# A third weight sum of a Winograd product made on VectorE instead of by a load and an accumulating DMA

## The reference, cut to what matters

```python
h = _rmsnorm(x, g_ffn[l])
z = _dwconv_centred(h @ w_up[l], conv_w[l], conv_b[l])      # w_up: 1024 x 5632
z_gate, z_val = jnp.split(z, [D_FF], axis=-1)               # D_FF = 2816, 22 tiles of 128
x = x + (jax.nn.silu(z_gate) * z_val) @ w_down[l]
```

## Time and profile before

| | us |
|---|---|
| median of 3 runs | 1084.41 (1084.4 to 1085.13) |
| the profiled execution | 1084.41 |
| its span, first to last instruction | 1082.6 |
| PE busy | 1071.1 (99%) |
| PEld busy | 941.5 (87%) |
| POOL busy | 636.1 (59%) |
| DVE busy | 596.6 (55%) |
| ACT busy | 557.4 (51%) |

### The profile page before, as it was taken

The page is one execution under the profiler, slowest core; times in us unless marked ns, Lnnn a source line. Parts: engine busy times, 40 slices in busy tenths (PEclk is TensorE's granted clock), DMA queues, the critical chain, the costliest instruction groups (busy, mean ns, idle before and its releaser), DMA issues.

```text
span 1082.6 us, 18370 instructions
## 1 busy us (share of the span) xinstructions
PE 1071.1 (99%) x6492; PEld 941.5 (87%) x6492; DVE 596.6 (55%) x922; ACT 557.4 (51%) x772; POOL 636.1 (59%) x314
## 2 busy tenths in 40 slices
PE   9999999999999999999999999999999999999997
PEld 7788888888899989998878888888879998899987
DVE  4735755677146730676636359556741776136664
ACT  7835334545266623675548344445444675257651
POOL 5333334344799948995634333434458995789940
PEclk9999999999999999999999999999999999999999
DMA  8232123232999459972522221322349973898512
GB/s 306 96 97 79 59 65 110 78 112 83 247 232 241 119 158 248 208 167 96 173 81 89 79 79 60 97 97 78 101 141 266 231 177 98 241 207 221 133 56 79
DMA packets 45156, 151.12 MB, mean 140 GB/s; under 512 B 5264, under 2 KB 8080, under 8 KB 45072
## 3 DMA queue, kind: packets, MB, share of 16 engines
q1 hardware_dynamic: 35152, 115.42, 32.9%
q0 software_dynamic: 9216, 33.56, 16.9%
q10 hardware_dynamic: 704, 1.07, 0.3%
HBM read 131.15 MB, written 2.10 MB: 123 GB/s over the span
## 4 chain that ended last, share of the span: by engine, by line
PE 70%; POOL 9%; DVE 9%; DMA 4%; ACT 3%; issue 3%; DVEq 0%; ACTq 0%; SPq 0%; POOLq 0%
PE acc L1482 12%; PE acc L1483 12%; PE acc L1484 12%; POOL w_lo L464 8%; PE acc L1796 7%; PE acc L1799 7%; PE acc L1798 7%; DVE arena L1304 3%; PE acc L1608 3%; PE acc L1610 3%; PE acc L1609 3%; DMA mixer_sb<-w_raw 2%; DMA w_raw<-slabs 2%; ACT arena L805 2%; DVE sides L1295 1%
## 5 line engine op out<-in xcount | busy, mean ns | idle before, releaser
L474 POOL TENSOR_TENSOR w_lo<-w_raw,w_hi 128x1024 fp32r<-128x1024 f32 x108 | 262.2, 2448 | 331.8 <-ACT w_hi L541 329.0
L464 POOL TENSOR_TENSOR w_lo<-w_raw,w_hi 128x1024 fp32r<-128x1024 f32 x72 | 190.7, 2752 | 37.4 <-ACT w_hi L824 24.7
L1482 PE MATMUL acc<-feat_hi,w_hi 128*128 128x512 f32 (+1 forms) x496 | 190.1, 383 | 1.6 <-DVE x L1246 1.5
L1483 PE MATMUL acc<-feat_lo,w_hi 128*128 128x512 f32 (+1 forms) x496 | 189.7, 382 | 0.0
L1484 PE MATMUL acc<-feat_hi,w_lo 128*128 128x512 f32 (+1 forms) x496 | 189.6, 382 | 0.0
L541 ACT ACTIVATE w_hi<-w_raw 128x1024 fp32r<-128x1024 f32 x102 | 107.9, 1063 | 139.8 <-PE acc L1484 103.4
L1798 PE MATMUL acc<-xg_lo,w_hi 128*128 128x256 f32 x512 | 144.9, 283 | 0.0
L1799 PE MATMUL acc<-xg_hi,w_lo 128*128 128x256 f32 x512 | 144.9, 283 | 0.0
L1796 PE MATMUL acc<-xg_hi,w_hi 128*128 128x256 f32 x512 | 144.9, 283 | 0.0
L1482 PE MATMUL acc<-xg_hi,w_hi 128*128 128x512 f32 x352 | 139.6, 397 | 0.0
L1483 PE MATMUL acc<-xg_lo,w_hi 128*128 128x512 f32 x352 | 137.1, 389 | 0.0
(11 more groups left out here) (179 smaller groups left out, 2136.6 us busy)
## 6 DMA issues: line engine op xcount, KB each, us to landing
w_raw<-slabs SPq DMA_DIRECT2D x166, 512.0 KB, 3.5
mixer_sb<-slabs SPq DMA_DIRECT2D x16, 512.0 KB, 5.6
w_raw<-slabs POOLq DMA_DIRECT2D x16, 512.0 KB, 6.7
arena<-slabs SPq DMA_DIRECT2D x16, 512.0 KB, 4.9
arena<-slabs POOLq DMA_DIRECT2D x16, 512.0 KB, 7.1
second_s<-slabs SPq DMA_DIRECT2D x8, 512.0 KB, 6.5
mixer_sb<-w_raw POOLq DMA_DIRECT2D x8, 512.0 KB, 8.8
w_raw<-mixer_sb POOLq DMA_DIRECT2D x8, 512.0 KB, 6.6
```

The lines of the kernel that those rows point to most:

```text
L464: pool.tensor_tensor(w_lo[:, w], source, w_hi[:, w].bitcast(F32), ALU.subtract).then_inc(lo_done, 1)
L474: pool.tensor_tensor(w_lo[:, w], w_raw[:, w], w_hi[:, w].bitcast(F32), ALU.subtract).then_inc(lo_done, 1)
L1482: pe.matmul(out, wh, ah, start=first, stop=False)
L1483: pe.matmul(out, wh, al, start=False, stop=False)
```

## The change

S2 is no longer made by DMA. SP's second load of A11 (`load_s2`) and POOL's accumulating DMA (`add_s2`) go, with the semaphores `s2_loaded` and `s2_added`. In their place DVE adds `raw1` and `raw0` into `s2_raw` with one `tensor_tensor` per quad, 16 in all, and increments `s2_done`. It waits until S1 is summed, A11 is loaded, and the quad two before has done with the same S2 buffer. POOL's `add_s3`, which overwrites A11, now waits for `s2_done`, and ACT's `high_s2` does too.

```diff
--- before.py
+++ after.py
@@ -271,8 +271,7 @@
         s1_added = [sem(f"s1_added{i}") for i in range(2)]
         s3_added = [sem(f"s3_added{i}") for i in range(2)]
         s4_added = [sem(f"s4_added{i}") for i in range(2)]
-        s2_loaded = [sem(f"s2_loaded{i}") for i in range(2)]
-        s2_added = [sem(f"s2_added{i}") for i in range(2)]
+        s2_done = sem("s2_done")
         e12_done, t1_raw_done, t2_done, t_raw_done = (sem("e12_done"), sem("t1_raw_done"), sem("t2_done"),
                                                       sem("t_raw_done"))
         t_hi_done, t_ready = sem("t_hi_done"), sem("t_ready")
@@ -341,20 +340,13 @@
                 def load_a22(s):
                     sp.dma_start(raw(3), block(s, 3)).then_inc(a22_loaded, 16)
 
-                def load_s2(s):
-                    sp.dma_start(s2_raw[s % 2], block(s, 0)).then_inc(s2_loaded[s % 2], 16)
-
                 def load_down(m):
                     sp.dma_start(raw(m % RING), block(KP, m)).then_inc(raw_loaded[m % RING], 16)
 
                 for j, load in enumerate((load_a11, load_a21, load_a12, load_a22)):
                     low_of(L, p, 0, j - RING)
                     load(0)
-                    if j == 0:
-                        sp.wait_ge(t1_ready, L + 1)
-                        load_s2(0)
                 load_a21(1)
-                load_s2(1)
                 load_a11(1)
                 load_a12(1)
                 for s in range(2, KP):
@@ -365,7 +357,6 @@
                     low_of(L, p, s - 2, S3_)
                     load_a11(s)
                     low_of(L, p, s - 2, S4_)
-                    load_s2(s)
                     load_a12(s)
                 low_of(L, p, KP - 2, S2_)
                 load_down(1)
@@ -480,23 +471,16 @@
                 pool.dma_start(raw1[s % 2], block_of(L * NS + first_slab(p, s) + 3),
                                accum_op=ALU.add).then_inc(s1_added[s % 2], 16)
 
-            def add_s2(L, p, s):
-
-                count = 16 * ((L * QUADS + p * KP + s) // 2 + 1)
-                pool.wait_ge(s2_loaded[s % 2], count)
-                pool.wait_ge(s1_added[s % 2], count)
-                pool.dma_start(s2_raw[s % 2], raw1[s % 2], accum_op=ALU.add).then_inc(s2_added[s % 2], 16)
-
             def add_s3(L, p, s):
 
                 low_done(L * NU + first_unit(p, s) + A11_)
+                pool.wait_ge(s2_done, L * QUADS + p * KP + s + 1)
                 pool.dma_start(raw0[s % 2], block_of(L * NS + first_slab(p, s) + 1),
                                accum_op=ALU.add).then_inc(s3_added[s % 2], 16)
 
             def add_s4(L, p, s):
 
                 low_done(L * NU + first_unit(p, s) + A12_)
-                pool.wait_ge(s2_added[s % 2], 16 * ((L * QUADS + p * KP + s) // 2 + 1))
                 pool.dma_start(raw2[s % 2], s2_raw[s % 2], accum_op=ALU.add).then_inc(s4_added[s % 2], 16)
 
             def low_quad(L, p, s):
@@ -509,8 +493,6 @@
                 low(n + A12_, raw2[s % 2])
                 add_s4(L, p, s)
                 low(n + S2_, s2_raw[s % 2])
-                if s < KP - 1:
-                    add_s2(L, p, s + 1)
                 low(n + A22_, raw(3))
                 low(n + S3_, raw0[s % 2])
                 low(n + S4_, raw2[s % 2])
@@ -525,7 +507,6 @@
                     low(n - 2, raw(2))
                     add_s1(L, p, 0)
                     low(n - 1, raw(3))
-                    add_s2(L, p, 0)
                     for s in range(KP):
                         low_quad(L, p, s)
                     down = at + first_unit(p, KP)
@@ -840,7 +821,7 @@
                     high(first_unit(p, s) + A12_, raw2[s % 2])
 
                 def high_s2(p, s):
-                    act.wait_ge(s2_added[s % 2], loads(p, s))
+                    act.wait_ge(s2_done, L * QUADS + (p * KP + s + 1))
                     high(first_unit(p, s) + S2_, s2_raw[s % 2])
 
                 def high_a22(p, s):
@@ -1318,6 +1299,17 @@
                 def halves(bank):
                     return bank.rearrange("p (r s) -> p r s", r=2)
 
+                def add_s2(p, s):
+
+                    count = 16 * (L * (QUADS // 2)) + 16 * ((p * KP + s) // 2 + 1)
+                    dve.wait_ge(s1_added[s % 2], count)
+                    dve.wait_ge(a11_loaded[s % 2], count)
+                    if p * KP + s > 1:
+                        before = p * KP + s - 2
+                        dve.wait_ge(s4_added[before % 2], 16 * (L * (QUADS // 2)) + 16 * (before // 2 + 1))
+                        dve.wait_ge(lo_done, L * NU + (first_unit(before // KP, before % KP) + S2_ + 1 + RING))
+                    dve.tensor_tensor(s2_raw[s % 2], raw1[s % 2], raw0[s % 2], ALU.add).then_inc(s2_done, 1)
+
                 def add_c11(p, s):
                     dve.wait_ge(acc_ready, L * NU + (first_unit(p, s) + A12_ + 1))
                     dve.wait_ge(copied, quad_at(p, s) * 4 + 2)
@@ -1364,7 +1356,7 @@
                 def quad_low(p, s, b):
                     feat_low(FIRST_TILES + p * KT + 2 * s + b, 2 * s + b, b)
 
-                def convolve(p, s):
+                def convolve(p, s, between):
 
                     add_c12(p, s)
                     scale(p, s, 0)
@@ -1373,6 +1365,7 @@
                     taps(p, s, 0)
                     scale(p, s, 3)
                     taps(p, s, 2)
+                    between()
                     gate(p, s, 0)
                     taps(p, s, 3)
                     quad_low(p, s, 0)
@@ -1381,7 +1374,9 @@
 
                 def quad_step(p, s):
                     if s:
-                        convolve(p, s - 1)
+                        convolve(p, s - 1, (lambda: add_s2(p, s + 1)) if s < KP - 1 else (lambda: None))
+                    else:
+                        add_s2(p, 1)
                     add_c11(p, s)
                     add_c22(p, s)
                     add_c21(p, s)
@@ -1397,12 +1392,18 @@
                 dve.wait_ge(t1_hi_done, L + 1)
                 dve.tensor_tensor(xg12_lo, t1_raw.rearrange("p (k s) -> p k s", k=KP), xg12_hi.bitcast(F32),
                                   ALU.subtract).then_inc(t1_ready, 1)
+                for m in range(RING + 1):
+                    down_add(N_DOWN, m)
                 for p in range(FULL_PARTS):
-                    for m in range(KT):
+                    add_s2(p, 0)
+                    for m in range(RING + 1, KT):
                         down_add(first_unit(p) - KT, m)
                     for s in range(KP):
                         quad_step(p, s)
-                    convolve(p, KP - 1)
+                    convolve(p, KP - 1, lambda: None)
+                    if p < FULL_PARTS - 1:
+                        for m in range(RING + 1):
+                            down_add(first_unit(p, KP), m)
 
                 def last_down(m):
```

## The result

| | before | after |
|---|---|---|
| median, us | 1084.77 (1084.4 to 1086.14, 4 runs) | 1096.7 (1095.78 to 1098.7, 4 runs) |
| profiled execution, its span | 1084.41, 1082.6 | 1098.84, 1097.0 |

The ratio is 1.0109 [1.0093, 1.0125]. The prediction said 1081.4 and at most 1083.4, so it was wrong in sign.

The account below looks back on a forecast made before the run. PE, busy 99%, was taken as the bound, losing 3.73 us to POOL's late chain in the first parts; gains of 2.0 us (layer 0) and 1.03 (layer 1) took 1084.41 to 1081.4, with an 8-in-10 range of 1080.5 to 1083.4.

Parts of the forecast that it names:

- DVE, waiting, got in between two subtractions that stood back to back: Reading of POOL's pair at 157.69, the second held 0.45 us; used to price an add at 0.93 us of POOL.
- of at most 2.38 plus 1.23: Longest wait of the gate behind the add in quads 2 and 3: one subtraction, 2.38 us, plus the add, 1.23.
- the chain's 9.51 us: POOL's subtractions in a quad, from the chain: 9.51 / 4 = 2.38 us each, seven per quad of 20.88.
- My sum with the rule "in full", 1082.7: POOL pays every DVE add in full, without credit for DMA issue slots: 0.63 us more per layer, 1082.7.
- The cover: Time from the gate's end to its reader on ACT, 4.34 us, against the gate's wait behind the add.
- what happens when it is gone: If the gate's cover of 4.34 us were gone, ACT's next high halves would be late.
- Rival C: Slower: each add holds POOL for a whole subtraction's length; 1087.2 to 1093.0, about 1090; chance 0.05.
- Quad 0: Start of each first part: POOL's chain gains 2.49 us in layer 0 and 1.51 in layer 1.
- Two adds outside of `convolve`: S2 of quads 0 and 1: quad 0's add free, quad 1's up to 0.93 us, taken as 0.3.
- POOL's accumulating DMAs landed sooner: With two of nine transfers gone, S1 of quad 1 expected early; transfers in quad 0 landing in under 9 us.
- The expected gain of 3.0 us: Whole kernel: 2.0 us in layer 0 and 1.03 in layer 1, both in the first parts.
- four adds per layer inside of `convolve`: S2 of quads 2 and 3: each add costs POOL 0.93 us for 0.84 that went, 0.18 lost over two quads.

Follow-up runs that it names:

- experiment 10: Kernel before the change, plus a half-width two-SBUF-input DVE add in `convolve` for quads 2 and 3, result unread; 1116.42 us, ratio 1.0297 to the kernel before.
- experiment 2: Changed kernel, but in quads 1 and 2 POOL waits for its own last result ahead of three subtractions; 1082.55 us, ratio 0.9977 to the kernel before.
- experiment 7: Changed kernel, but in quads 1 and 2 POOL waits for its own last result only ahead of S4's subtraction; 1085.39 us, ratio 1.0012 to the kernel before.
- experiment 3: Changed kernel, but DVE adds S2 only for quads 0 and 1; quads 2 and 3 use load and DMA again; 1081.48 us, ratio 0.9973 to the kernel before.
- (1): Changed kernel, but the adds inside `convolve` read their second input from PSUM (wrong sum); 1080.93 us, ratio 0.9963 to the kernel before.
- 9: Experiment 5's kernel, but in quads 1 and 2 POOL waits for its S1 subtraction before the next S1's DMA issue; 1090.24 us, ratio 1.006 to the kernel before.
- experiment 5: Changed kernel, with the add moved to the end of `convolve`, behind the second tile's low half; 1088.21 us, ratio 1.0026 to the kernel before.
- experiment 4: Changed kernel, with the add inside `convolve` one instruction later, behind the gate of tile 0; 1105.56 us, ratio 1.0198 to the kernel before.
- experiment 6: Changed kernel, with the add inside `convolve` moved ahead, between tile 2's scaling and tile 0's taps; 1129.05 us, ratio 1.0414 to the kernel before.

## Why the prediction was wrong

**The step that failed.** It is the sentence "DVE, waiting, got in between two subtractions that stood back to back", and what was drawn from it: a wait "of at most 2.38 plus 1.23". The pair at 157.69 belongs to a different loop (line 474), in which most subtractions start behind a wait; no DMA issue of POOL stands beside this pair. Its second subtraction did not wait, but was begun only 0.04 us before the first ended:

```profile
157.69 2.40 POOL L474 TENSOR_TENSOR w_lo<-w_raw,w_hi 128x1024 fp32r<-128x1024 f32 x1 [7.92 <-ACT w_hi L541]
...
160.05 2.85 POOL L474 TENSOR_TENSOR w_lo<-w_raw,w_hi 128x1024 fp32r<-128x1024 f32 x1
```

In the quads, line 464, where DMA issues stand among the subtractions, half of the leads were 0.5 us or more already in the kernel before. The adds were held for up to 8.21 us there, and up to 9.40 in experiment 10. The page of the kernel before shows the difference in the lengths:

```profile
L474 POOL TENSOR_TENSOR w_lo<-w_raw,w_hi 128x1024 fp32r<-128x1024 f32 x108 | 262.2, 2448 | 331.8 <-ACT w_hi L541 329.0
L464 POOL TENSOR_TENSOR w_lo<-w_raw,w_hi 128x1024 fp32r<-128x1024 f32 x72 | 190.7, 2752 | 37.4 <-ACT w_hi L824 24.7
```

The same operation takes 2448 ns in the one and 2752 in the other. The spacing in a run is 2.37 (316.31, 318.68), so those of 2752 overlap the one before them: they were begun ahead of their turn. I had divided the chain's 9.51 us by four and had not asked why the single rows say 2.7. In experiment 2, behind a gap, the row says 2.42 again (316.83).

**The rule of the Trainium skill** (SBUF — State Buffer, "Who interferes with whom") says who excludes whom, and on that the traces agree: with one input in PSUM the add took 1.22 us. It has the port held until the end of the instruction that issued first. These runs show more than that: the add begun at 317.54 was kept out by the subtractions of 318.68 and 321.04 too, which began after it. My sum with the rule "in full", 1082.7, was too mild for the same reason.

**The cover.** The prediction took 4.34 us as cover, from the end of the gate to ACT's `feat_high`. That was the slack of ACT in the kernel before. In the changed kernel ACT's high halves came sooner and it was idle in front of the gate from 319.97 on, so ACT had hardly any. The slack that counts is that of PE: the gate came 7.26 us later and PE lost 2.89 - 0.12 = 2.77, so 4.49 were absorbed, and 4.68 beside the add of 8.21. The 4.34 was thus about right, but by luck. The prediction's sentence on what happens when it is gone was right. Five of eight adds exceeded it. In experiment 7 the adds of 4.84 to 5.92 us went over it by little, and PE's longest wait was 1.1 us.

**The clock** was no term of the sum, and no reason was given for leaving it out. It came to about 4 us of the 15.

**Rival C** named the right sign and the right first place (POOL's port) but the wrong victim. It had POOL held by DVE; it was DVE held by POOL, and through DVE, ACT and PE. Its number, about 1090, was 7 too low, and it had 0.05.

**What was right.** Quad 0: the spacing from the last tile's addition to the first C12 is 309.62 - 289.47 = 20.15, and was 21.05. Two adds outside of `convolve` cost next to nothing, the one of quad 1 took 2.46 and 2.52 us in the two first parts. POOL's accumulating DMAs landed sooner. In the page's list of DMA issues, where the medians before were 6.7 and 7.1:

```profile
w_raw<-slabs POOLq DMA_DIRECT2D x16, 512.0 KB, 5.4
...
arena<-slabs POOLq DMA_DIRECT2D x16, 512.0 KB, 5.5
```

The expected gain of 3.0 us is there: experiment 3, with those adds alone, ran 4.0 us under the kernel before in its profiled execution (1080.42 against 1084.41) and its ratio to that kernel is 0.9973. The error is all in the four adds per layer inside of `convolve`.

**Shown and not shown.** Shown: that the second SBUF input is the cause (1), that the adds alone suffice (10), that a wait of POOL ends the hold (2, 7, 9), and that neither a DMA issue nor the end of a single subtraction does so by itself (5 and the changed kernel). The way from the late gate to PE over ACT is read from the timelines. That POOL keeps the port by instructions begun ahead of their turn is inferred: the lead goes with the hold in every case, but no run changes the lead alone.

## What to carry to other kernels

Before a two-input SBUF operation is put on DVE beside a busy POOL, look at how POOL's instructions there follow one another. Where their records overlap by 0.2 us or more, as in the runs here with DMA issues in them, the operation lasts to POOL's next wait. Where they overlap by 0.1 or less, it got in at the end of the current instruction. A version with both benefits keeps such adds where POOL waits anyway (experiment 3), reads one input from PSUM, or puts a wait for POOL's own result into its run (0.9977 of the kernel before, experiment 2). And an instruction placed ahead of one that an in-order engine waits for is to be costed at its longest, since a break of PE is also paid in its clock.

## What the hardware showed unexpectedly

- POOL kept the SBUF port through runs of subtractions: up to 8.21 us for an add of 1.22, and 9.40 for one of half the width. A DMA issue in the run did not end it when begun 0.37 us ahead (6.80 us, experiment 5) and did when begun 0.07 ahead (2.69 us, same kernel). A gap of 0.08 us always did (experiment 2).
- The stall can feed on itself or end itself. In the changed kernel the add ended because it had starved POOL by way of ACT; when ACT was spared that (experiment 4), the add grew from 7.26 to 9.09 us.
- In the changed kernel PE's granted clock fell to half behind breaks of 3.65 and 3.31 us, for 6.8 and 3.4 us, and did not behind those of 2.89, 2.56 and 2.54. The length of the break does not decide alone: in experiment 5 the clock stayed full behind one of 3.02, and in experiment 10 it fell at one of 2.58 and at one of 2.13.
- The place of such an add decides more than its size. A few instructions earlier on DVE (experiment 6) the kernel took 4.1% more than before, in place of 1.1%.
